# Five blocks of 1, 2, 2, 2 and 1 tiles in place of four of two, with a new pace for the expert gathers

## The reference, cut to what matters

```python
scores = jnp.einsum('thpd,hpnd->thpn', q, keys)
top_s, top_i = lax.top_k(scores, PEER_TOPK)             # 16 of 128, for each half of the key
cand = top_s[:, :, 0, :, None] + top_s[:, :, 1, None, :]
best_s, best_pos = lax.top_k(cand..., PEER_TOPK)        # 16 of 256
u = jnp.take(u_tab, e_blk, axis=0)                      # (tokens, 128, 1024)
act = jax.nn.gelu(jnp.einsum('td,tkd->tk', h_blk, u), approximate=False) * g_blk
vv = jnp.take(v_tab, e_blk, axis=0)
y = jnp.einsum('tk,tkd->td', act, vv)
h = layernorm(ALPHA * h + y)
```

## Time and profile before

| | us |
|---|---|
| median of 3 runs | 3895.95 (3892.21 to 3900.37) |
| the profiled execution's own time | 3910.97 |
| its span in the profile | 3909.0 |
| PE busy | 2510.5 (64%) |
| DVE busy | 2368.6 (61%) |
| POOL busy | 2263.7 (58%) |
| ACT busy | 519.2 (13%) |
| DMA | 1300.60 MB, 333 GB/s over the span |

### The profile page before, as it was taken

The page is one execution under the profiler, slowest core; times in us unless marked ns, Lnnn a source line. Parts: engine busy times, 40 slices in busy tenths (PEclk is TensorE's granted clock), DMA queues, the critical chain, the costliest instruction groups (busy, mean ns, idle before and its releaser), DMA issues.

```text
span 3909.0 us, 36881 instructions
## 1 busy us (share of the span) xinstructions
PE 2510.5 (64%) x11992; PEld 1546.1 (40%) x11992; DVE 2368.6 (61%) x5585; ACT 519.2 (13%) x1187; POOL 2263.7 (58%) x2086
## 2 busy tenths in 40 slices
PE   6889775356896876657796886656697750033354
PEld 5666663242554643433554653423373320000011
DVE  4153799765447877655448977655535878844400
ACT  2121220121102311111101311111100000000000
POOL 1000255456565676767665666767765678777775
PEclk8889887676798997867798997877798885555577
DMA  4313587579999999999999999999999999999998
GB/s 141 112 57 136 208 309 279 199 248 356 366 407 350 383 405 368 340 346 365 358 413 345 387 407 377 350 352 364 335 413 382 392 401 332 369 387 406 409 410 347
DMA packets 372174, 1300.60 MB, mean 333 GB/s; under 512 B 39953, under 2 KB 69649, under 8 KB 366865
## 3 DMA queue, kind: packets, MB, share of 16 engines
q0 software_dynamic: 294912, 1073.87, 71.8%
q1 hardware_dynamic: 71312, 211.80, 14.5%
q10 hardware_dynamic: 5760, 12.59, 0.8%
HBM read 1285.12 MB, written 12.98 MB: 332 GB/s over the span
## 4 chain that ended last, share of the span: by engine, by line
PE 32%; DVE 20%; POOL 18%; DMA 13%; issue 10%; DVEq 4%; ACT 3%; SPq 0%; POOLq 0%; ACTq 0%
PE bank L1313 12%; DMA ring<-in_ev,idxT 10%; POOL ring L636 9%; DVE ring L972 9%; POOL ring L648 8%; PE bank L1302 7%; PE bank L1323 3%; PE bank L1523 3%; PE bank L1577 3%; DMA arena<-d_rows 1%; PE bank L1500 1%; DVE nm L1154 1%; DMA ring<-in_eu,eidx 1%; PE bank L1363 1%; DVE arena L1148 1%
## 5 line engine op out<-in xcount | busy, mean ns | idle before, releaser
L636 POOL DMA_INDIRECT ring<-in_eu,eidx x1024 | 1171.6, 1144 | 1161.9 <-DVE eidx L1269 428.3
L972 DVE CUSTOM_DVE_ANT_0 ring<-ring,h_cur 128x1024 f32<-128x1024 f32 x1024 | 1213.8, 1222 | 232.1 <-DMA ring<-in_eu,eidx 228.4
L648 POOL DMA_INDIRECT ring<-in_ev,idxT x1024 | 1080.3, 1055 | 456.0 <-issue 290.0
L1302 PE MATMUL bank<-ring,wide 128*32 128x512 f32 x4096 | 707.6, 825 | 558.6 <-DMA ring<-in_ev,idxT 546.2
L1313 PE MATMUL bank<-arena,wslot 128*128 128x256 f32 (+1 forms) x3248 | 750.2, 389 | 54.7 <-ACT arena L749 38.8
L1313 PEld LDWEIGHTS bank<-arena,wslot 128*128 128x128 f32 (+1 forms) x3248 | 623.6, 194 | 221.7 <-issue 119.5
L1302 PEld LDWEIGHTS bank<-ring,wide 128*32 128x32 f32 x4096 | 143.8, 135 | 959.7 <-issue 938.6
L1323 PE MATMUL bank<-arena 128*128 128x128 f32 x1408 | 227.6, 323 | 47.1 <-ACT arena L795 34.2
L1323 PEld LDWEIGHTS bank<-arena 128*128 128x128 f32 x1408 | 208.2, 232 | 81.3 <-ACT arena L795 44.4
L1523 PE MATMUL bank<-arena 128*128 128x64 f32 x528 | 114.6, 398 | 171.7 <-ACT arena L830 171.7
L1523 PEld LDWEIGHTS bank<-arena 128*128 128x128 f32 x528 | 105.9, 303 | 185.2 <-ACT arena L830 185.2
(11 more groups left out here) (229 smaller groups left out, 2472.1 us busy)
## 6 DMA issues: line engine op xcount, KB each, us to landing
wslot<-in_w_pq SPq DMA_DIRECT2D x64, 576.0 KB, 7.7
wslot<-in_w_mix SPq DMA_DIRECT2D x24, 1536.0 KB, 9.8
wslot<-in_w_qkv SPq DMA_DIRECT2D x48, 512.0 KB, 6.5
wslot<-in_w_fqk SPq DMA_DIRECT2D x32, 512.0 KB, 7.5
wslot<-in_w_out SPq DMA_DIRECT2D x8, 2048.0 KB, 10.4
ring<-in_eu,eidx POOLq DMA_INDIRECT x1024, 7.0
ring<-in_ev,idxT POOLq DMA_INDIRECT x1024, 8.5
wslot<-in_w_z SPq DMA_DIRECT2D x16, 512.0 KB, 6.4
```

Of the source, the lines that this page charges most:

```text
L636: pool.indirect_dma_start(out=ring[:, UPOS[k] % NR, :], out_offset=None, in_=eu, in_offset=bass.IndirectOffsetOnAxis(ap=eidx[:, n % (2 * T ...
L648: pool.indirect_dma_start(out=ring[:, VPOS[k] % NR, :], out_offset=None, in_=ev, in_offset=bass.IndirectOffsetOnAxis(ap=idxT[:, n % (2 * T ...
L972: dve.tensor_tensor_reduce(out=row, in0=row, in1=h_cur[:, n % 3, :], scale=1.0, scalar=0.0, op0=ALU.mult, op1=ALU.add, accum_out=dots[:, n ...
L1302: last = pe.matmul(BY[k][32 * j:32 * j + 32, :], wide32[:, at:at + 32], ring[:, VPOS[4 * q + j] % NR, k * 512:(k + 1) * 512], start=(m == ...
```

## The change

Blocks get a size of their own, `SIZES = [1, 2, 2, 2, 1]`. All stages take the width of their block; block 0 has one tile, so its delta is one chunk and its attention 9 steps, and so has block 4. All tensors of a block are views of the same memory with the block's own shape. All weights are now loaded five times. The numbers of chosen experts keep four tiles' worth of room, shifted by one (`(n + 1) % 4`).

`pace()` is new: the dots and the sum of dots and V rows are drawn as lines between marks, each mark a unit with a number of dots and a number of both; V rows fill whatever dots can't (they are limited to finished tiles). Up to the end of choose of block 0 at most 64 dots. During the last choose, V rows as before. The values that follow from the new functions, beside those of before (dots / V rows done when the unit is reached):

| unit | before | after |
|---|---|---|
| prod of block 1 | 108 / 0 | 72 / 0 |
| mix of block 1 | 200 / 64 | 128 / 64 |
| choose of block 1 | 240 / 104 | 128 / 112 |
| prod of block 2 | 345 / 204 | 246 / 128 |
| mix of block 2 | 455 / 316 | 357 / 256 |
| choose of block 2 | 496 / 360 | 384 / 280 |
| prod of block 3 | 601 / 460 | 504 / 384 |
| mix of block 3 | 729 / 584 | 640 / 524 |
| choose of block 3 | 768 / 636 | 640 / 580 |
| prod of block 4 | | 760 / 640 |
| mix of block 4 | | 869 / 720 |
| choose of block 4 | | 896 / 760 |
| end of the last choose | 768 / 768 | 896 / 896 |

At the start the two constants of the second norm are loaded later (at `prod` of block 0), and the activations and the first weights are asked for before the other constants.

```diff
-T = 256
-NB = SEQ // T
-TT = T // P
+SIZES = [1, 2, 2, 2, 1]
+NB = len(SIZES)
+TT = max(SIZES)
+T = TT * P
+START = [sum(SIZES[:b]) for b in range(NB + 1)]
+WID = [n * P for n in SIZES]
+BLOCK = [b for b in range(NB) for _ in range(SIZES[b])]
...
+FIRST = 64
+MARKS = [(("prod", 1, 0), 72, 72), (("att", 1, 0), P, 144), (("top", 1, 0), P, 240)]
...
-    gates = [("lev", LEVELS * (TT - 1) + l) for l in range(1, LEVELS)] + [(kind, TT - 1) for kind in ("ws", "o", "og")]
+    gates = [("lev", l) for l in range(1, LEVELS)] + [(kind, 0) for kind in ("ws", "o", "og")]
...
+HALF = {"sm": 0.6, "conv": 0.6, "z": 0.6, "fqk": 0.6, "fv": 0.6, "prod": 0.8, "mix": 0.7, "top": 0.5, "cand": 0.55, "sel": 0.55}
...
 def share(kind, b):
-    return SHARE[kind] * (1.0 + 0.7 * b if kind == "att" else 1.0)
+    return (SHARE[kind] * (HALF.get(kind, 1.0) if SIZES[b] == 1 else 1.0)
+            * (1.0 + 0.35 * START[b] if kind == "att" else 1.0))
...
-    total = sum(share(kind, b) for kind, b, i in UNITS[first + 1:alone])
+    every = P * START[NB - 1]
+    marks = [(first + 1, FIRST, FIRST)] + [(UNITS.index(u), d, a) for u, d, a in MARKS] + [(alone, every, 2 * every - P - LAG)]
...
         if kind == "sel":
-            ready, lately = T * b + TOPK * i, 0
+            ready, lately = P * START[b] + TOPK * i, 0
...
-            want = min(want, P - 8)
+            want = both = min(want, FIRST)
         else:
-            run += share(kind, b) if n < alone else 0.0
-            want = base + round((T * (NB - 1) - base) * run / total)
+            m = max(k for k in range(len(marks) - 1) if marks[k][0] <= n)
+            (a, d0, b0), (z, d1, b1) = marks[m:m + 2]
+            run = sum(share(k, c) for k, c, _ in UNITS[a:min(n + 1, z)]) / sum(share(k, c) for k, c, _ in UNITS[a:z])
+            want, both = d0 + round((d1 - d0) * run), b0 + round((b1 - b0) * run)
         dots.append(max(dots[-1], min(want, ready, dots[-1] + 8)))
+        whole, edge, step = dots[-2] // P * P, P * (toks[-1] // P + 1), 4
+        if n > alone:
+            begin = toks[alone + 1]
+            both, step = dots[-1] + begin + round((every - begin) * (n - alone) / (last - alone)), 8
+        toks.append(max(toks[-1], min((both - dots[-1]) // 4 * 4, whole, edge, toks[-1] + step)))
...
-            for k in range(2):
-                sp.dma_start(ln2B[:, k, :], ln[2 + k:3 + k, :].to_broadcast([P, D])).then_inc(s_cst, 16)
...
             def prod(b, c):
+                if c == 0 and b == 0:
+                    for k in range(2):
+                        sp.dma_start(ln2B[:, k, :], ln[2 + k:3 + k, :].to_broadcast([P, D])).then_inc(s_ln2, 16)
...
-                    block_mm(B[3 * j + 1][:, 0:T], w, oTg, nk=4)
-                    block_mm(B[3 * j][:, 0:T], w, oTf[b], nk=4, k0=4).then_inc(s_yb[j], 1)
+                    block_mm(B[3 * j + 1][:, 0:WID[b]], w, oTg[b], nk=4)
+                    block_mm(B[3 * j][:, 0:WID[b]], w, oTf[b], nk=4, k0=4).then_inc(s_yb[j], 1)
```

More of the change, by code:

```diff
@@ L29 @@
 LEVELS = 6
-MA = (FH // 2) * 2 * TT
+MA = [FH * n for n in SIZES]
+M0 = [FH * n for n in START]
 ARENA = 16070
@@ L33, with delta, attend, merge @@
 LAG = 8
+FIRST = 64
+MARKS = [(("prod", 1, 0), 72, 72), (("att", 1, 0), P, 144), (("top", 1, 0), P, 240)]
 PROJECT = ([("sm", 0)] + [("conv", c) for c in range(13)] + [("z", 0), ("z", 1), ("rT", 0)]
            + [("fqk", c) for c in range(8)] + [("fv", 0), ("fv", 1)])
[L39 to L43, removed]
+def delta(b):
+    units = []
+    for c in range(SIZES[b]):
+        units.append(("prod", c))
+        for l in range(LEVELS):
+            units.append(("lev", LEVELS * c + l))
+            if c and l == 1:
+                units.append(("og", c - 1))
+        units += [("wu", c), ("ws", c), ("o", c)]
+    return units + [("og", SIZES[b] - 1)]
+def attend(b):
+    return [("att", m) for m in range(MA[b] + 1)] + [("ot", 0)]
+def merge(b):
+    return ([("mix", i) for i in range(8)] + [("wo", i) for i in range(2 * SIZES[b])]
+            + [("ln", tt) for tt in range(SIZES[b])])
 CHOOSE = [u for i in range(PH) for u in (("top", 2 * i), ("top", 2 * i + 1), ("cand", i), ("sel", i))] + [("idx", 0)]
@@ L64, in order @@
         units += [(k, 0, j) for k, j in here]
-    units += [(kind, 0, i) for kind, i in ATTEND[-1:] + MERGE]
+    units += [(kind, 0, i) for kind, i in attend(0)[-1:] + merge(0)]
     for b in range(NB):
         if b:
-            units += [(kind, b, i) for kind, i in DELTA + ATTEND + MERGE]
+            units += [(kind, b, i) for kind, i in delta(b) + attend(b) + merge(b)]
         after = PROJECT if b + 1 < NB else []
@@ L117, in pace @@
     dots += [P * NT] * 48
-    for s in range(1, len(dots)):
+    for s in range(len(toks), len(dots)):
         edge = P * (toks[-1] // P + 1)
         ready = dots[s] - P - LAG if dots[s] < P * NT else toks[-1] + 4
[L121 to L125, removed]
         if toks[-1] % P == 0 and dots[s - 1] < edge:
             ready = toks[-1]
-        toks.append(max(toks[-1], min(ready // 4 * 4, edge, toks[-1] + step)))
+        toks.append(max(toks[-1], min(ready // 4 * 4, edge, toks[-1] + 4)))
     assert toks[-1] == P * NT and toks[-5] == P * NT
@@ L339, in build, with in_ring @@
-        sg0 = ring[:, 9:13, :].rearrange("p a (i k t) -> p (a i) k t", i=2, k=2)
+        xTm = Region(ARENA - KB * T).each(lambda n: (KB, n * P))
+        W0 = WID[0]
+        assert SIZES[0] == 1
+        def in_ring(place, word, *shape):
+            n = 1
+            for m in shape:
+                n *= m
+            v = ring[:, place, word:word + n]
+            return v.rearrange("p (a b) -> p a b", a=shape[0]) if len(shape) == 2 else v
+        xTs[0] = xTm[0] = in_ring(0, 0, KB, W0)
@@ L352, in build @@
         r = Region(after_fq)
-        mixT = r.take(KB, T)
+        mixT = r.each(lambda n: (KB, n * P))
         h1 = r.take(TT, D)
@@ L1001, in sm_ @@
                 dve.drain()
-                dve.tensor_tensor(L, L, rows, ALU.add)
+                dve.tensor_tensor(L, L, rows_, ALU.add)
                 dve.tensor_scalar(A, V, 0.0, None, ALU.max)
@@ L1376, in rT @@
                 if b:
-                    pe.wait_ge(s_natev[1], 4 * b + 1)
-                for tt in range(TT):
-                    last = pe.transpose(B[5][:, tt * ROWS:(tt + 1) * ROWS], rows[:, tt * P:(tt + 1) * P],
+                    pe.wait_ge(s_natev[1], evicted(b, 1, 1))
+                for tt in range(SIZES[b]):
+                    last = pe.transpose(B[5][:, tt * ROWS:(tt + 1) * ROWS], rows[b][:, tt * P:(tt + 1) * P],
                                         ident[0:ROWS, 0:ROWS])
@@ L1410, in prod @@
                 part = slice(c * P, (c + 1) * P)
-                qn, kn, v = (qkvS[:, 4 * k:4 * k + 4, part] for k in range(3))
+                qn, kn, v = (qkvS[b][:, 4 * k:4 * k + 4, part] for k in range(3))
                 if c == 0:
```

586 lines of the change are left out of this document (298 added, 288 removed).

## The result

The changed kernel takes **4151.2 us** (median of 4 runs, 4142.9 to 4160.1) beside 3898.2 for the kernel before (4 runs, 3892.2 to 3903.0): a ratio of 1.065, 95% interval 1.0623 to 1.0677. The forecast was 4005 with a range to 4110. The direction was right, the size was not: 253 us slower and not 109. The profiled execution took 4160.1 us, its span is 4158.3.

A forecast was written before the change was run, and what follows sets the result against it. The prediction held nothing is gathered until 419 us and bytes bind from 1028 us on; block 2 reached at 1166 plus 2854 for the rest gave 4020, adjusted to 4007, stated as 4005 us (2.8% slower), range 3850 to 4110.

The forecast's parts named there:

- the start: Block 0, halved to one tile: 250 us instead of 419, bounds 230 and 310.
- the last four terms: From block 4 to the end: delta and attention 299 us, merge 135, choose 203, tail 368.
- the cross-check: From block 2 on, 1030 MB must move; ending at 3909 would need 375 GB/s, the forecast's sum means 361.
- Rival 1: From block 2 on, delta and attention's fixed parts are latency that more gathers fill: 384 GB/s, 3835 us; chance 0.27.
- choose 2 and 3: Choose of blocks 2 and 3: gathers plus fixed part, 373 and 316 us, plus 5 and 6 for DVE: 378 and 322.
- rival 3: Choose of blocks 2 and 3 as a DMA-bound then a DVE-bound half: 425 and 369 us, total 4100; chance 0.15.
- Choose 1: Choose of block 1: 294 us of DVE work, some 15 of 309 better hidden, so 310 us (295 to 325).
- Choose 0: First choose, one tile: 164 us of DVE work over busy share 0.895, 183 us instead of 309 (170 to 205).
- Delta and attention 1: Block 1's delta and attention: one tile less in attention and 42 dots less, 265 us instead of 300 (250 to 290).
- Merge 3: Merge of block 3: 56 gathers, all V, 14 groups against 10: 166 us.
- Delta and attention 3: Block 3's delta and attention: 276 gathers at 1.28 us plus a fixed 92, 445 us.
- The fifth load: Loading all weights a fifth time, with other added loads: 46.5 MB, at 408 GB/s 114 us.

The follow-up runs named there:

- e5_spread_only: Changed kernel with all gathers per stage kept, only the V rows inside choose of blocks 2 and 3 spread evenly: 4104.9 us, ratio 1.0509.
- e6_lump_before: Kernel before with the V rows of block 2's choose moved as early as allowed, into its first half: 3947.9 us, ratio 1.011.
- e4_shift_v: Changed kernel with 88 V rows of tile 0 moved from block 1's attention and merge into its choose: 4083.5 us, ratio 1.0478.
- e3_smooth_choose: Changed kernel with more pace marks, so that V rows are not taken at the start of choose: 4049.7 us, ratio 1.0386.
- e8_even_marks: Changed kernel with marks for little V beside attention, U rows kept for merges, both even in choose: 4032.8 us, ratio 1.0336.
- e11_changed_again: The changed kernel itself, unaltered, run again on a chip where the kernel before is slower: 4242.6 us, ratio 1.0587.

## Why the prediction was wrong

**Right.** The bytes (1347.86 MB for 1347); the start (252 for 250); the last four terms (1014 us for 1005 in sum); merge 2; the frame of the argument as well: from the start of block 2 on 2936 us at 350 GB/s are 1027 MB, for 1030 in the cross-check. That check said that 3909 needs 375 GB/s and that my sum meant 361. The kernel reached 350. The merges of blocks 2 and 3 show a DMA share of 0.91 and 0.87 and PE at 0.89 and 0.97, as put, and the second halves of choose idle DMA behind DVE, as put. Rival 1 falls: the two delta stages of two tiles from block 2 on took 1.28 us per gather plus 71 and plus 112, and the rate stayed below 375. Of the signs given, two came out late: block 2 is reached at 1222 us for 1166, the last choose at 3590 for 3449. The start isn't to blame for either.

**The step that failed** is the term for choose 2 and 3: "Dots wait for the `sel` of their own block, so the second half of each is set by DVE; I add 5 and 6". The mechanism was named and its size was not worked out there, though it was in rival 3, with 425 and 369; measured are 406 and 365. With 28 and 43 us these two stages are half of what the sum lacked. Rival 3's sum, 4100, was the nearest of the cases, and I gave it 0.15 on the ground that "units lag behind the stream by up to a ring". The runs show in its place that the halves follow one another: the lag of up to 15 rows hides little of it. Of 49 us of DVE work (44 us of compares and the time between them), 11.5 reach the end when they are added to the first half (9 by the ratios) and 51.8 when added to the second (52 by the ratios). The order of the V rows alone is worth 46 us here (`e5_spread_only`) and 45 in the kernel before (`e6_lump_before`). Whether a longer ring would carry the lag over was not run. The row against my term stood in the earlier trace rows: choose before had 0.98 because U and V were mixed to the end of it, and I carried its fixed part of 83 to 88 us to a stage with another mix.

**Choose 1** (+24) is the same error in another form. DVE's work came out to the microsecond, 294 us for 294. I let it fill 0.95 of the stage, because "some 15 of 309 can be hidden better than at first"; it filled 0.88, between the 0.85 and the 0.92 of the two DVE-bound halves above. By the 0.895 of the first choose before the term would have been 328.

**Choose 0** (+13): DVE 172.7 us for 164, at a busy share of 0.88 and not 0.895. I took one tile as half of two. It isn't, as the compare of the selection shows, before with two tiles, and then after with one:

```profile
L1258 DVE TENSOR_TENSOR arena<-arena,iota 128x512 f32<-128x512 f32 x16 | 11.1, 693 | 1.2
```

```profile
L1322 DVE TENSOR_TENSOR arena<-arena,iota 128x256 f32<-128x256 f32 x16 | 6.8, 427 | 1.2
```

One tile costs 0.62 of two in this operation, and the work without dots was 98 us and not 79 + 10. Three wide operations of the selection, this one among them, account for some 3 of these 9 us; the rest I did not split up. The Trainium skill (VectorE: DVE Perf Modes, the section on the TRN2 errata) says that an operation that reads SBUF pays a fixed latency whatever its length. The trace agrees: 256 columns more cost 266 ns, so some 160 of the 427 ns don't depend on the length. I had weighed no such rule for the term that halves DVE's work.

**Delta and attention 1** (+23): I took dots and one tile off and nothing for V. 60 V rows stand in that attention with 51.3 us of PE; with 12 of them it is 28 us shorter (`e4_shift_v`). The term's upper bound, 290, held.

**Merge 3** (-14) and merge 1 (-6) were costed too dear. For merge 3 I added PE time for 14 groups of V rows to a merge that had PE idle.

**Delta and attention 3** (+27): it had 281 gathers for 276, which is 6 us. The traces show where the other 21 lie. In the pace of the changed kernel V's rows reach 512 in this attention, the end of a tile. V of the next tile may start only with all its dots done, and for four steps of the attention there are only dots. The DMA engines run half empty there:

```profile
2570.00:2595.00 25.00, 9.84 (x35) 7.63 (x35) 15.11 (x27) 3.78 (x8) 10.40 (x8) 0.50 0.62 204
2595.00:2620.00 25.00, 13.71 (x48) 10.12 (x47) 14.05 (x29) 4.35 (x8) 12.02 (x9) 0.50 0.54 175
```

The marks of `e3_smooth_choose`, `e4_shift_v` and `e8_even_marks` don't stop V there, and their stage takes 448, 451 and 395 us with 276, 281 and 236 gathers: 1.28 us for each and 95, 91 and 93 besides, close to the 92 of my term. The changed kernel and `e5_spread_only`, which stop, take 483 us with 286 and 490 with 288, so 117 and 121 besides. This is read from traces of runs made for another purpose; no run changes the stop alone.

**The fifth load**, 114 us in the argument, is not what went wrong, but it was too dear: 36 MB of it measured 44 to 56 us where the rate gives 88. The other half found room; the choose stages of the changed kernel, not DMA-bound throughout, have some. `e8_even_marks`, which fills them, pays 130 us over the kernel before, with 46.5 MB at 365 GB/s being 127. That these two are the same, and that the room was in the choose stages, is only argued.

## What to carry to other kernels

Where two kinds of work alternate inside a stage (transfers that need no compute before they are issued, and transfers that wait for it), price each half of the stage by its own engine: a stage that has idle time on average can be bound throughout. Filling idle bandwidth with work of the first kind helps only where none of the second kind waits for its turn later in the same stage, so spread it and don't lump it. A stream that may not cross a border until other work is done (here V at the end of a tile) leaves a gap where it meets that border, so look where in the stages the borders fall. And a busy share that an engine reaches when it is the bound (here 0.85 to 0.92 for DVE) belongs in every term in which it is the bound.

## What the runs showed of the chip

Two of the chips ran the kernel before in 4007.0 and 4008.3 us, the others in 3898 to 3903, with no other change. I compare the changed kernel on the chip of its result with `e11_changed_again` on a slower one. The first 1220 us are the same on both (261 GB/s). What follows takes 2936 us on the one and 3005 on the other. Its last stretch, in which the DMA engines are nearly full, is 564 us long on the first chip, and the same work takes 583 on the slower one:

```profile
3594.00:4158.00 564.00, 206.86 (x1316) 70.05 (x1315) 261.57 (x640) 15.63 (x36) 395.19 (x382) 0.71 0.97 375
```

```profile
3642.00:4225.00 583.00, 215.03 (x1315) 73.02 (x1315) 262.29 (x640) 15.50 (x36) 386.11 (x382) 0.70 0.95 363
```

So the cost of a gather was 3% higher there. Each chip was used in one session only, so that this is the chip and not the session isn't shown. The changed kernel loses less than the kernel before, 91 us for 110, and its ratio was 1.065 on the one and 1.0587 on the other; its lower DMA share from block 2 on (0.93 for 0.97) fits this.
